# A hybrid encoder step on one core: attention steps moved by units, the router taken token tile by token tile, and a ring of twelve weight buffers for the experts

## The chip, the cores and the metric

One NeuronCore of one Trainium2 chip runs the whole step; the other cores are idle. The metric is the device time of one execution in microseconds (us), the median of several.

## The reference

One layer of a streaming encoder on 512 prompt tokens and 32 sample tokens (544 rows, five token tiles: four of 128 and one of 32), D = 1024, everything in float32.

```python
h = rms_norm(x, p['norm_mix'])
z = h @ p['w_in']                       # qa ka va ra code | qb kb vb | ga gb
...
o_a = rms_norm(o_a, p['gla_norm']) * silu(ra)
u_a = o_a @ p['w_proj_a']
...                                     # 8 heads, softmax1 - lam * softmax2
u_b = o_b @ p['w_proj_b']
mix = sigmoid(ga) * u_a + sigmoid(gb) * u_b
x = x + mix @ p['w_out']
x = x + hmoe(rms_norm(x, p['norm_ffn']), ...)
```

hmoe picks for each token one of 4 groups and in it the best 2 of 4 experts, and adds their weighted outputs (silu(x @ w_gate) * (x @ w_up)) @ w_down, with w_gate and w_up of 1024 x 512 and w_down of 512 x 1024. The outputs are the normalised rows, the new keys and values, and the recurrent GLA state.

## The kernel before, in words

**Arithmetic.** Each fp32 product is three products of reduced-precision parts: every operand is split into a high part, on ScalarE (ACT), and a low part, on VectorE (DVE). three_products (lines 1012 to 1014) does hi x hi, hi x lo and lo x hi on TensorE (PE).

**Units.** layout_of_units writes the projections as a list of units in the order qa, ka, va, ra, qb, kb, vb, ga, gb, pa, pb, wo. A unit is one PSUM bank of output: 24 products of 272 columns for a feature-major stage (128 features by half of the tokens), or two token tiles by 256 columns for va, ra, vb and wo. Weights come in tiles of 256 columns (128 for ga, gb, pa, pb) into a ring of two, and take_apart splits them (lines 697 and 1372). Unit u uses bank u % 3 and waits until unit u - 3 has been evicted.

**Hooks.** hook(u, what) hangs a step behind unit u. Every engine walks the same list of units, and does its part of each hooked step at that place of its own program; so the order on each engine follows from the hook table. Hooked are the GLA steps (gla_in, gla_o, gla_out for token tile i), kout (key rows), the 32 attention slots (head k // 4, query block k % 4) with their later parts up to slot 35, the sample's keys, scores, softmax and values (keys, sscore, soft, mixp, probs, svalue, snorm, sturn), the split of the two attention outputs (oa, ob), the sigmoids (sig) and the first router steps.

**Router.** After wo the rows x2 are normalised (h2, line 1499) and stored to h2_rows in DRAM (POOL, line 643), transposed and multiplied with the router weights. When all five tiles' logits are there, DVE works out group, experts, rank and slot for all tiles at once in some sixty small operations (lines 1609 to 1687), with rank sums (1236, 1238) and a slot table (1245) on PE. From slot_i, POOL gathers each expert's 128 rows by an indirect DMA (line 656).

**Experts.** Each of 16 experts has six weight parts of 1 MB: gate 0 and 1, up 2 and 3, down 4 and 5. SP (the load queue) loads each into the one of six raw slots that belongs to its kind, when DVE has made e_lo of the part before it there. ACT makes e_hi (899, three buffers), DVE e_lo (1696); POOL makes e_lo of the first two parts (652). PE's body(r) does GU (gate and up products) of expert r, AT (transpose of hh) and Dn (down products) of expert r - 1, and XT, the transposes of expert r + 1's rows. ACT copies the result to yo and stores it to y_rows; at the end each token's two rows are gathered (yg), weighted and added, and the last norm follows.

Of the kernel before, what the change touches and what calls it, by code (L numbers as in the profile page):

```python
# [38 lines left out]
NBLK = NE + NOVF  # L39
PARTS, PART, PBUF = 6, KC * FE // 2, 3  # L40
# [4 lines left out]
SLOTS = 4 * DH  # L45

# [5 lines left out]
def layout_of_units():  # L52
# [4 lines left out]
              ("ga", "w_in", C_GA, D), ("gb", "w_in", C_GB, D), ("pa", "w_proj_a", 0, D), ("pb", "w_proj_b", 0, D),  # L57
              ("wo", "w_out", 0, D)]
    tiles, kinds, nth = [], [], []
    for kind, name, col, width in stages:  # L60
        wide = P if kind in NARROW else WC
        for n in range(width // wide):
            tiles.append((name, col + n * wide, wide))
            kinds.append(kind)
            nth.append(n)
# [6 lines left out]
    for n, kind in enumerate(kinds):  # L72
        token_major = kind in ("va", "ra", "vb", "wo")

        parts = [(i, 0) for i in range(0, NTILE, 2)] if token_major else [(f, h) for f in range(tiles[n][2] // P) for h in range(2)]
        for m, (a, b) in enumerate(parts):
            if kind == "ra":
                eng = "A"
            elif kind in ("pa", "pb", "wo"):
# [5 lines left out]
            h = 2 * nth[n] + m - 4  # L85
            if kind == "pa" and 0 <= h < DH:
                add("AD"[h % 2], tile=None, kind="ox", nth=h, a=0, b=0, first=False, last=False, token_major=False)
    return tiles, kinds, units


def build(nc, x_prompt, x_sample, cache_k, cache_v, state_gla, norm_mix, w_in, w_decay, b_decay, gla_norm, w_proj_a,
# [16 lines left out]
    h2_rows = nc.dram_tensor("h2_rows", (NT, D), F32)  # L108
    y_rows = nc.dram_tensor("y_rows", (NBLK * CAP, D), F32)
    h2_rows, y_rows = h2_rows.ap(), y_rows.ap()  # L110

    ctx = ExitStack()
    with ctx:
# [16 lines left out]
        g_diff_s = small[:, 21:22]  # L130
# [51 lines left out]
        dist_s = at("dist_s", AT_X + 4224, [P, PAST + TS])  # L182
        dist = at("dist", AT_X + 8448, [P, TP])
        kbS = at("kbS", AT_X + 10496, [P, DH, TS])
        obs = at("obs", AT_X + 11520, [P, DVB])
        obq = at("obq", AT_X + 12032, [P, DVB])
        head_st = at("head_st", AT_X + 12544, [P, 3, 4 * DH])
        att_st = at("att_st", AT_X + 12928, [P, 4, 8])
# [1601 lines left out]
```

## Time and profile before

| | us |
|---|---|
| median of 3 runs | 1170.91 (1169.93 to 1171.38) |
| the profiled execution's own time | 1172.25 |
| its span in the trace | 1170.3 |
| PE busy | 1034.7 (88%) |
| DVE, ACT, POOL busy | 639.5, 541.4, 141.3 |
| mean granted clock of PE | 0.945 |

The trace is of one execution. A wait is idle time of an engine in front of an instruction, with what ended it. The granted clock is PE's, as a share of full speed. GLA runs until some 300 us, attention from 417 to 585, the sample's attention until some 720, wo from 721, the router from 776, the experts from 830 to 1133.

### The profile page before, as it was taken

The page shows a single profiled execution, that of the slowest core. Times are in us where ns is not written, and L with a number is a line of the kernel's source. Part 1 is how long each engine was busy: PE and PEld are TensorE (multiplying, and loading weights), DVE is VectorE, ACT ScalarE, POOL GpSimd, SP SyncE. Part 2 cuts the span into 40 slices and gives each one's busy share as a digit, 9 for nine tenths or more (in the row PEclk, how much of TensorE's full clock was granted, in tenths as well). Part 3 has the DMA queues.
Part 4 walks back from the last instruction along what each step waited for, and adds up shares of the span by engine and source line. Part 5 has one row for each costly group of instructions (what it writes and reads, how often), then busy time and mean ns, then how long its engine had stood idle before and what let it go on. Part 6 is the DMA issues. An engine that isn't in the chain of part 4 may idle for free.

```text
span 1170.3 us, 17496 instructions
## 1 busy us (share of the span) xinstructions
PE 1034.7 (88%) x7174; PEld 943.2 (81%) x7174; DVE 639.5 (55%) x919; ACT 541.4 (46%) x717; POOL 141.3 (12%) x138
## 2 busy tenths in 40 slices
PE   3999999999999989999789798992599999999940
PEld 2999999887999978888678698992478888888830
DVE  5223821343221146767644465237569889889826
ACT  6225622332122144544644522142367787787722
POOL 3200000200000033422111100003100101100003
PEclk9999999999999999999899898995799999999975
DMA  7863545326364485564343345412489999999736
GB/s 154 255 83 64 67 78 74 55 41 103 64 83 91 77 123 81 47 81 73 122 131 109 99 141 172 189 72 77 159 292 413 412 414 414 413 414 414 278 111 229
DMA packets 125514, 198.01 MB, mean 169 GB/s; under 512 B 10864, under 2 KB 72304, under 8 KB 125440
## 3 DMA queue, kind: packets, MB, share of 16 engines
q1 hardware_dynamic: 112336, 149.37, 48.3%
q0 software_dynamic: 10176, 36.97, 8.6%
q10 hardware_dynamic: 2928, 10.62, 2.3%
q8 instruction: 55, 0.90, 0.3%
q14 instruction: 19, 0.16, 0.0%
HBM read 174.40 MB, written 22.54 MB: 168 GB/s over the span
## 4 chain that ended last, share of the span: by engine, by line
PE 83%; DVE 6%; ACT 4%; DMA 3%; issue 2%; POOL 0%; ACTq 0%; DVEq 0%; POOLq 0%
PE ps L1012 24%; PE ps L1014 23%; PE ps L1013 23%; PE ps L997 5%; PE ps L1143 2%; PE ps L1129 2%; DVE x L1759 1%; DMA ring<-in_w_in_dram 1%; PE ps L1108 1%; PE ps L1076 1%; PE ps L1092 1%; ACT sqa L750 1%; DVE ra L1437 1%; DMA out_dram<-vb 1%; PE ps L1107 1%
## 5 line engine op out<-in xcount | busy, mean ns | idle before, releaser
L1696 DVE TENSOR_TENSOR e_lo<-raw,e_hi 128x2048 fp32r<-128x2048 f32 x94 | 215.0, 2288 | 47.9 <-ACT e_hi L899 47.3
L899 ACT ACTIVATE e_hi<-raw 128x2048 fp32r<-128x2048 f32 x96 | 184.1, 1918 | 70.0 <-PE ps L1014 52.0
L1012 PE MATMUL ps<-h_hi,w_hi 128*128 128x272 f32 x640 | 191.7, 300 | 3.9 <-DVE h_lo L1361 3.9
L1014 PE MATMUL ps<-h_hi,w_lo 128*128 128x272 f32 x640 | 186.9, 292 | 0.0
L1013 PE MATMUL ps<-h_lo,w_hi 128*128 128x272 f32 x640 | 186.7, 292 | 0.0
L1372 DVE TENSOR_TENSOR w_lo<-ring,w_hi 128x2048 fp32r<-128x2048 f32 (+1 forms) x44 | 81.7, 1856 | 105.5 <-ACT w_hi L697 105.5
L697 ACT ACTIVATE w_hi<-ring 128x1024 fp32r<-128x1024 f32 (+1 forms) x60 | 87.2, 1453 | 107.6 <-PE ps L1014 98.1
L1012 PE MATMUL ps<-w_hi,h_hi 128*128 128x256 f32 x480 | 136.1, 284 | 0.0
L1013 PE MATMUL ps<-w_lo,h_hi 128*128 128x256 f32 x480 | 135.7, 283 | 0.0
L1014 PE MATMUL ps<-w_hi,h_lo 128*128 128x256 f32 x480 | 134.7, 281 | 0.0
L1012 PEld LDWEIGHTS ps<-h_hi,w_hi 128*128 128x128 f32 x640 | 123.1, 192 | 5.5 <-DVE h_lo L1361 4.1
L1013 PEld LDWEIGHTS ps<-h_lo,w_hi 128*128 128x128 f32 x640 | 123.2, 192 | 0.2
L1014 PEld LDWEIGHTS ps<-h_hi,w_lo 128*128 128x128 f32 x640 | 122.8, 192 | 0.0
L1012 PE MATMUL ps<-e_hi,x_hi 128*128 128x512 f32 x256 | 104.9, 410 | 7.4 <-DVE hh L1705 5.0
L1014 PE MATMUL ps<-e_hi,x_lo 128*128 128x512 f32 x256 | 101.6, 397 | 0.0
L1013 PE MATMUL ps<-e_lo,x_hi 128*128 128x512 f32 x256 | 101.4, 396 | 0.0
L1012 PEld LDWEIGHTS ps<-w_hi,h_hi 128*128 128x128 f32 x480 | 90.4, 188 | 1.5 <-ACT va L873 1.1
L1014 PEld LDWEIGHTS ps<-w_hi,h_lo 128*128 128x128 f32 x480 | 90.8, 189 | 0.0
L1013 PEld LDWEIGHTS ps<-w_lo,h_hi 128*128 128x128 f32 x480 | 90.2, 188 | 0.0
L1012 PEld LDWEIGHTS ps<-e_hi,x_hi 128*128 128x128 f32 x256 | 49.2, 192 | 18.3 <-DVE hh L1705 5.4
L1014 PEld LDWEIGHTS ps<-e_hi,x_lo 128*128 128x128 f32 x256 | 49.0, 191 | 10.9
L1013 PEld LDWEIGHTS ps<-e_lo,x_hi 128*128 128x128 f32 x256 | 49.4, 193 | 9.0
(349 smaller groups left out, 2020.7 us busy)
## 6 DMA issues: line engine op xcount, KB each, us to landing
raw<-in_w_gate_dram SPq DMA_DIRECT2D x32, 1024.0 KB, 8.8
raw<-in_w_up_dram SPq DMA_DIRECT2D x32, 1024.0 KB, 9.6
raw<-in_w_down_dram SPq DMA_DIRECT2D x32, 1024.0 KB, 8.3
ring<-in_w_in_dram SPq DMA_DIRECT2D x24, 1024.0 KB, 9.3
ring<-in_w_in_dram SPq DMA_DIRECT2D x16, 512.0 KB, 8.6
y_rows<-yo ACTq DMA_DIRECT2D x16, 512.0 KB, 6.0
y_rows<-att POOLq DMA_DIRECT2D x8, 512.0 KB, 13.6
kraw<-in_cache_k_dram POOLq DMA_DIRECT2D x8, 512.0 KB, 8.2
```

The costliest lines, as they stand in the source:

```text
L697: act.activation(piece(w_hi, n), piece(ring, n), ACT.Copy).then_inc(s_hi, 1)
L750: step(act.activation(sqa[0:n], ps[0:n, 5 + h // 2, DV * (h % 2):DV * (h % 2) + DV], ACT.Square, accum_out=stat[0:n, 16 + h:17 + h]))
L899: act.activation(e_hi[:, buf], raw[:, slot], ACT.Copy).then_inc(s_ehi, 1)
L997: last = pe.transpose(out, src, ident[0:ident_n, 0:ident_n])
L1012: pe.matmul(out, left[0], right[0], start=first, stop=False)
L1013: pe.matmul(out, left[0], right[1], start=False, stop=False)
L1014: return pe.matmul(out, left[1], right[0], start=False, stop=final)
L1076: last = pe.matmul(ps[0:n, 5, (NG + NE) * i:(NG + NE) * (i + 1)], h2T[:, i % 2, c, 0:n], wr[:, c], start=c == 0, stop=c == KC - 1)
L1129: last = pe.matmul(ps[:, 3 + a, 0:w], qbT[r, h, P * q:P * q + P], kbT[r, h, 0:w], start=True, stop=True)
L1143: last = pe.matmul(ps[:, 6 + h % 2, DVB * q:DVB * q + DVB], pT[:, k % 2, P * c:P * c + P], vb[:, c, DVB * h:DVB * h + DVB], start=c == 0, ...
L1372: dve.tensor_tensor(piece(w_lo, n), piece(ring, n), piece(w_hi, n).bitcast(F32), ALU.subtract).then_inc(s_lo, 1)
L1696: dve.tensor_tensor(e_lo[:, buf], raw[:, slot], e_hi[:, buf].bitcast(F32), ALU.subtract).then_inc(s_elo, 1)
```

## The change

The first part moves hooks. The second rewrites wo and the router. The third changes the weight ring.

```diff
-            hook(units_of["qb"][3 * i + 1], "gla_out", i)
-            hook(units_of["vb"][2 * i + 1], "kout", i)
-        hook(units_of["vb"][-1], "dist")
+                hook(units_of["qb"][3 * i - 1], "gla_out", i - 1)
+            hook(units_of["vb"][2 * i], "kout", i)
+        hook(units_of["vb"][8], "dist")
...
-        for k in range(SLOTS):
-            hook(gates[k], "slot", k)
+        for k in range(SLOTS + 3):
+            hook((units_of["vb"][-3:] + gates)[k], "slot", k)
+        hook(gates[-2], "oa", 0)
+        hook(gates[-1], "slot", SLOTS + 3)
+        hook(gates[-1], "oa", 1)
         hook(gates[-1], "sig", 0)
-        hook(pa[0], "slot", SLOTS + 2)
-        hook(pa[1], "slot", SLOTS + 3)
-        hook(pa[2], "roots")
+        hook(pa[0], "roots")
```

The sample's steps are spread anew over the 16 units of pa, with the keys in pairs of heads; the sigmoid of gb moves from pa's last unit to pa[12], ob's pieces to pa[10], [11], [13], [14]. dist_s is made later. DVE's wait for the store of vb moves from slot 0 to the rows of head 0 (slot 7). pb's first unit waits for 4 pieces of ob_lo and its second for 6, where the first waited for 6.

wo becomes ten units of one token tile by 512 columns, in the order of WO_ORDER, with w_out in four pieces of 1 MB that have buffers of their own. The router's steps hang behind these units, tile by tile; a step in mid_hooks runs on PE in the middle of the unit.

```diff
+WO_ORDER = [(0, 0), (1, 0), (2, 0), (0, 1), (1, 1), (2, 1), (3, 0), (3, 1), (4, 0), (4, 1)]
...
+        for u, *steps in ((wo[3], ("sq", 0), ("h2", 0)),
+                          (wo[4], ("sq", 1), ("turn", 0), ("logits", 0), ("route", 0), ("h2", 1)),
+                          (wo[5], ("sq", 2), ("turn", 1), ("logits", 1), ("rank", 0), ("slots", 0), ("route", 1), ("h2", 2)),
+                          (wo[6], ("turn", 2), ("logits", 2), ("rank", 1), ("slots", 1), ("route", 2)),
+                          (wo[7], ("sq", 3), ("rank", 2), ("slots", 2), ("h2", 3), ("early", 0)),
+                          (wo[8], ("turn", 3), ("logits", 3), ("route", 3)),
+                          (wo[9], ("sq", 4), ("rank", 3), ("turn", 4), ("slots", 3), ("logits", 4), ("root", 4), ("route", 4), ("rank", 4),
+                           ("h2", 4), ("slots", 4), ("totals", 0))):
...
+            def route(i, n):
...
+                step(dve.max(best[0:n, i], masked))
+                step(dve.max_index(which[0:n], best[0:n, i], masked))
...
+            def slots(i, n):
+
+                dve.wait_ge(s_rank, i + 1)
+                step(dve.tensor_tensor(rt[0:n, 4], ps[0:n, 7, 0:NE], iota_r[0:n], ALU.add))
...
-            for e in range(NE):
-                if e >= 2:
-                    pool.wait_ge(s_xt, e - 1)
-                gather(e, e % 2)
+                for k in range(2):
+                    pool.indirect_dma_start(x_rows, bass.IndirectOffsetOnAxis(slot_i[0:n, k, i:i + 1], 0), h2[i % 2][0:n],
+                                            None).then_inc(s_sc[i % 2], 16)
+
+            def block_in(e, slot):
+                pool.dma_start(xg[:, slot], x_rows[ROWS * e:ROWS * e + CAP]).then_inc(s_xg[slot], 16)
+
+            for i in range(2):
+                pool.wait_ge(s_sc[i], 32 * ((NTILE + 1 - i) // 2))
+            block_in(0, 0)
+            block_in(1, 1)
```

So the normalised rows are scattered, two indirect DMAs a tile, into x_rows in DRAM, where each expert has room for 640 rows (ROWS), and an expert's 128 rows are then one plain load. turn transposes x2 itself, not h2: norm_ffn's gain is multiplied into the router's weights once, for which a small load is added, and the root of the row comes in at route. x_rows is zeroed beforehand by 16 DMAs of 512 KB (the eight y_rows blocks were zeroed before too). What concerns overflowing experts and the final row numbers, overflow() and weights(), stands on DVE after the conversion of part (0, 2). POOL makes no e_lo any more.

```diff
-PARTS, PART, PBUF = 6, KC * FE // 2, 3
+PARTS, PART, PBUF, RAW = 6, KC * FE // 2, 3, 12
...
+            for seq, (e, j) in enumerate(in_order):
+                if seq == 5:
+                    sp.wait_ge(s_unit, wo[8] + 1)
+                elif seq == 9:
+                    sp.wait_ge(s_unit, wo[9] + 1)
+                elif seq >= RAW:
+                    sp.wait_ge(s_part, seq - RAW + 1)
+                load_part(e, j, seq % RAW)
...
-                    dve.tensor_tensor(e_lo[:, buf], raw[:, slot], e_hi[:, buf].bitcast(F32), ALU.subtract).then_inc(s_elo, 1)
+                    dve.tensor_tensor(e_lo[slot][:], raw[slot][:], e_hi[buf][:].bitcast(F32), ALU.subtract).then_inc(s_elo, 1)
```

Parts go through twelve slots in order. e_lo is written over the raw weights of its slot, and a slot is free again when PE has used the part (s_part). Part (0, 0) is converted behind wo[7] ("early").

Three places of the order. First, ScalarE from wo's last weights on; sq is the Square of a row tile, x2T and h2T copies of its transposes. Before:

```order
L697 ACTIVATE w_hi_51<-ring_49 128x2048 [waits s_unit,s_w1]
L821 ACTIVATE sq_123,stat<-x_118 128x1024 [waits s_evD]
L822 ACT_TABLE_LOAD
L822 ACTIVATE stat<-stat,eps 128x1 [waits s_act]
L821 ACTIVATE sq_123,stat<-x_118 128x1024 [waits s_evD]
L822 ACTIVATE stat<-stat,eps 128x1 [waits s_act]
L828 ACTIVATE h2T<-ps 128x1024 [waits s_h2x]
```

Now:

```order
L748 ACTIVATE wo_hi_129<-wo_raw_125 128x2048 [waits s_w1]
L870 ACTIVATE sq_134,stat<-x_119 128x1024 [waits s_evD]
L871 ACT_TABLE_LOAD
L871 ACTIVATE stat<-stat,eps 128x1 [waits s_act]
L870 ACTIVATE sq_134,stat<-x_119 128x1024 [waits s_evD]
L871 ACTIVATE stat<-stat,eps 128x1 [waits s_act]
L877 ACTIVATE x2T<-ps 128x1024 [waits s_h2x]
L870 ACTIVATE sq_134,stat<-x_119 128x1024 [waits s_evD]
L871 ACTIVATE stat<-stat,eps 128x1 [waits s_act]
L877 ACTIVATE x2T<-ps 128x1024 [waits s_lgm,s_h2x] x2
```

The order of squares and copies is the old one, but these steps now lie between wo's units and not behind them.

Second, ScalarE at the passage from gb to pa; mixT at L776 and L822 is sigmoid 0, head_st the roots, kcT the copies of sample keys. Before:

```order
L718 ACTIVATE oa_hi<-fmA 128x1088 x3
L855 ACTIVATE pT<-ps 128x512 [waits s_pvq,s_px]
L776 ACT_TABLE_LOAD [waits s_evD]
L776 ACTIVATE mixT<-mixT 128x2176 [waits s_evA]
L776 ACTIVATE mixT<-mixT 128x2176
L835 ACTIVATE ob<-ps 128x512 [waits s_row,s_pvq]
L697 ACTIVATE w_hi_51<-ring_49 128x1024 [waits s_unit,s_w0]
L787 ACTIVATE kcT<-ps 128x512 [waits s_kcx] x4
L779 ACT_TABLE_LOAD
L779 ACTIVATE head_st<-head_st,eps 128x32 [waits s_row]
```

Now:

```order
L894 ACTIVATE ob<-ps 128x512 [waits s_row,s_pvq]
L864 ACTIVATE oa_hi<-fmA 128x4x272 [waits s_unit,s_oaT]
L864 ACTIVATE oa_hi<-fmA 128x4x272
L822 ACT_TABLE_LOAD [waits s_evD]
L822 ACTIVATE mixT<-mixT 128x2176 [waits s_evA]
L822 ACTIVATE mixT<-mixT 128x2176
L825 ACT_TABLE_LOAD
L825 ACTIVATE head_st<-head_st,eps 128x32 [waits s_row]
L833 ACTIVATE kcT<-ps 128x512 [waits s_kcx] x2
L738 ACTIVATE w_hi_51<-ring_49 128x1024 [waits s_unit,s_w0]
```

The roots moved ahead of the key copies, and the last outputs of attention (pT, ob) ahead of sigmoid 0.

Third, DVE at the first expert. Before:

```order
L1686 CAST ovi<-ovb 128x8 [waits s_dve]
L1687 CAST ovi<-ov 128x1 [waits s_dve]
L1696 TENSOR_TENSOR e_lo<-raw,e_hi 128x2048 [waits s_ehi,s_elo,s_ovi]
L1700 TENSOR_TENSOR x_lo<-ps,x_hi 128x1024 [waits s_xhi]
L1696 TENSOR_TENSOR e_lo<-raw,e_hi 128x2048 [waits s_ehi]
L1700 TENSOR_TENSOR x_lo<-ps,x_hi 128x1024 [waits s_xhi]
```

Now, the last of 46 small operations that stand between e_lo(0, 2) and e_lo(0, 3):

```order
L1776 CAST ysl<-ybase 128x10 [waits s_dve]
L1724 TENSOR_REDUCE rs<-rs 128x5 [waits s_ge]
L1725 RECIPROCAL rs<-rs 128x5 [waits s_dve]
L1726 TENSOR_SCALAR rs<-rs 128x5 [waits s_dve]
L1727 RECIPROCAL rs<-rs 128x5 [waits s_dve]
L1728 TENSOR_TENSOR rs<-rs 128x5 [waits s_dve]
L1729 TENSOR_TENSOR rs<-rs 128x5 [waits s_dve]
L1610 TENSOR_TENSOR e_lo_153<-raw_141,e_hi_162 128x2048 [waits s_ehi,s_dve]
L1780 TENSOR_TENSOR x_lo<-ps,x_hi 128x1024 [waits s_xhi]
```

The overflow work moved from in front of e_lo(0, 2) to behind it.

## Rows read from the trace of the kernel before

**Rows 1.** Waits of TensorE (PE), whole span. Columns: us in total, times, longest us.
```profile
PE ps L1236 <- DVE chosen L1634: 13.3, 1, 13.3
PE ps L1245 <- DVE ysl L1677: 9.6, 2, 7.0
PE ps L997 <- DVE ra L1437: 7.6, 5, 2.6
...
PE ps L997 <- DMA xg<-h_rows,slot_i: 4.9, 1, 4.9
...
PE ps L1129 <- DVE att_st L1529: 3.1, 1, 3.1
```
**Rows 2.** Stretch; length; busy of PE, PEld, DVE, ACT, POOL; PE clock; DMA share; GB/s.
```profile
200.00:230.00 30.00, 27.40 (x196) 26.52 (x196) 9.53 (x17) 9.11 (x20) 6.27 (x15) 0.94 0.40 76
420.00:424.00 4.00, 4.00 (x22) 3.99 (x21) 1.65 (x8) 2.13 (x7) 2.31 (x1) 0.59 0.98 43
562.00:592.00 30.00, 22.13 (x127) 19.76 (x125) 15.03 (x25) 18.34 (x23) 4.41 (x5) 0.77 0.40 123
592.00:660.00 68.00, 61.14 (x653) 54.77 (x652) 38.22 (x77) 32.38 (x50) 7.03 (x8) 1.00 0.35 109
660.00:678.00 18.00, 10.85 (x69) 10.64 (x68) 5.20 (x12) 8.17 (x9) 5.43 (x16) 0.72 0.59 211
718.00:728.00 10.00, 6.86 (x36) 6.67 (x35) 4.49 (x7) 2.67 (x3) 0.00 (x0) 0.66 0.51 164
```
**Rows 3.** Chain that ended last: start us, us, what; wo to expert 4.
```profile
718.22 3.14 issue
...
821.69 4.31 DMA xg<-h_rows,slot_i
826.04 1.98 PE ps L997 x8
...
830.39 0.80 PE ps L1012
...
850.23 0.80 PE ps L1012
...
875.60 0.87 PE ps L997 x8
893.34 0.87 PE ps L997 x8
```
**Rows 4.** Expert stage: columns of rows 2, then ScalarE's (ACT) longest wait.
```profile
900.00:1080.00 180.00, 180.00 (x854) 149.44 (x853) 160.48 (x92) 144.81 (x103) 14.47 (x9) 1.00 1.04 413
...
ACT e_hi L899 <- PE ps L1014: 27.4, 43, 0.8
```
**Rows 5.** Lines, 552 to 800: busy us, mean ns of one | idle before.
```profile
L776 ACT ACTIVATE mixT<-mixT 128x2176 f32<-128x2176 f32 x2 | 3.9, 2014 | 0.0
...
L776 ACT ACT_TABLE_LOAD x2 | 2.6, 1283 | 0.0
```
**Rows 6.** Lines, 760 to 832 (router), same columns.
```profile
L1499 DVE SCALAR_TENSOR_TENSOR h<-x,stat,gffn 128x1024 f32<-128x1024 f32 x4 | 5.1, 1284 | 0.1
...
L821 ACT ACTIVATE sq<-x 128x1024 f32<-128x1024 f32 x4 | 4.2, 1051 | 18.7 <-DVE x L1571 18.7
...
L656 POOL DMA_INDIRECT xg<-h_rows,slot_i x3 | 3.1, 1021 | 21.5 <-DVE slot_i L1679 17.1 <-PE ps L997 4.2 <-issue 0.3
```
**Rows 7.** Lines, 900 to 1080 (experts), same columns.
```profile
L1696 DVE TENSOR_TENSOR e_lo<-raw,e_hi 128x2048 fp32r<-128x2048 f32 x62 | 141.8, 2288 | 19.5 <-ACT e_hi L899 19.2
...
L656 POOL DMA_INDIRECT xg<-h_rows,slot_i x9 | 14.5, 1608 | 145.0 <-PE ps L997 145.0
```
**Rows 8.** DMA issues: out<-in, queue, count, KB each, median us to landing.
```profile
h_rows<-h POOLq DMA_DIRECT2D x4, 512.0 KB, 2.9
```
**Rows 9.** Experts' end: columns of rows 2, then a wait of ScalarE.
```profile
1112.00:1133.00 21.00, 14.26 (x50) 10.70 (x48) 6.91 (x5) 5.99 (x6) 0.00 (x0) 0.76 0.33 126
...
ACT e_hi L899 <- DMA raw<-in_w_down_dram: 6.4, 2, 5.0
```

More of the change, by code:

```diff
@@ new lines, in build @@
+        e_lo = [at(f"e_lo{k}", a, [P, PART], F32R) for k, a in enumerate(raw_at)]
+        e_hi = [at(f"e_hi{k}", a, [P, PART], F32R) for k, a in enumerate((181248, 143360, AT_H))]
+        xg = at("xg", AT_H + 8192, [P, 2, D])
+        x_hi = at("x_hi", AT_H + 16384, [P, 2, KC, P], F32R)
+        x_lo = at("x_lo", AT_H + 24576, [P, 2, KC, P], F32R)
+        hh_hi = at("hh_hi", AT_H + 32768, [P, FE // P, P], F32R)
+        hh_lo = at("hh_lo", 189440, [P, FE // P, P], F32R)
+        hh = at("hh", 151552, [P, 2, FE])
@@ L380, in build @@
[L380 to L391 removed]
+            hook(pa[2 + h], "normed", h)
@@ L571, in _, with head_bias @@
                 pool.dma_start(dst.rearrange("t h d -> t (h d)"), kb_rows[0:n, i % 2]).then_inc(s_kst[i % 2], 16)
+            def head_bias(h):
+                pool.tensor_scalar(bias[:, h % 2, 0:TP], dist[:], 2.0 ** -(h + 1), None, ALU.mult).then_inc(s_bias, 1)
+            pool.wait_ge(s_bs, 1)
+            head_bias(0)
+            head_bias(1)
+            pool.wait_ge(s_bias, 2)
             emptied(pool, units_of["vb"][-1])
@@ L575, in _ @@
             pool.dma_start(new_v_s[0, 0].rearrange("t h d -> t (h d)"), vb[0:TS, 4]).then_inc(s_vst, 16)
-            def head_bias(h):
-                pool.tensor_scalar(bias[:, h % 2, 0:TP], dist[:], 2.0 ** -(h + 1), None, ALU.mult).then_inc(s_bias, 1)
             def load_keys(g, j):
@@ L671, in _ @@
             pool.wait_ge(s_exdone, 1)
+            pool.wait_ge(s_ovi, 2)
             for i, (t0, n) in enumerate(TILES):
@@ L888, in _ @@
                     act.activation(m_hi[:, f, HALF * b:HALF * b + HALF], tmpm[:, b], ACT.Copy).then_inc(s_mhi, 1)
-                if d["last"] and d["tile"] + RING < len(wtiles):
+                if d["last"] and d["tile"] + RING < first_wo:
                     take_apart(d["tile"] + RING)
@@ L1259, in GU @@
                     c, w = KC // 2 * (j % 2) + i, slice(FE * i, FE * i + FE)
-                    last = three_products(ps[:, j // 2], (x_hi[:, slot, c], x_lo[:, slot, c]), (e_hi[:, buf, w], e_lo[:, buf, w]),
+                    last = three_products(ps[:, j // 2], (x_hi[:, slot, c], x_lo[:, slot, c]), (e_hi[buf][:, w], e_lo[low][:, w]),
                                           c == 0, c == KC - 1)
@@ L1275, in Dn @@
                         w = slice(D * i + 512 * b, D * i + 512 * b + 512)
-                        last = three_products(ps[:, 6 + b], (hh_hi[:, c], hh_lo[:, c]), (e_hi[:, buf, w], e_lo[:, buf, w]),
+                        last = three_products(ps[:, 6 + b], (hh_hi[:, c], hh_lo[:, c]), (e_hi[buf][:, w], e_lo[low][:, w]),
                                               c == 0, c == FE // P - 1)
@@ L1596, in _ @@
                             dve.tensor_copy(dst, src).then_inc(s_ev["D"], 1)
-                if d["last"] and d["tile"] + RING < len(wtiles):
+                if d["last"] and d["tile"] + RING < first_wo:
                     take_apart(d["tile"] + RING)
```

754 lines of the change are left out of this document (400 added, 354 removed).

## Prediction

> **What bounds the kernel now.** I read TensorE's waits over the whole span first [rows 1], then the granted clock by stage [rows 2], the chain that ended last [rows 3] and the expert stage [rows 4]. TensorE is the engine to follow: in the expert stage it is busy for 180.00 of 180 us at full clock while ScalarE's conversions wait for it and no wait for a weight load shows [rows 4]. So time is to be had only where TensorE stands still, and just after, because a stretch with a stall also shows a lower clock: 0.77, 0.72 and 0.66 in the three stretches of the attention tail with most idle time, against 1.00 between two of them [rows 2]. I count a clock loss as busy time x (1 - granted clock) of such a row. The sum is made against the profiled execution, 1172.25 us: span 1170.3 and 1.95 around it, and 1.34 over the median of 1170.91.
>
> **Part 1, GLA.** gla_out(i) stands one unit after gla_o(i) and waits for VectorE's ra five times, 7.6 us together, at most 2.6 [rows 1]. From the expert stage a product of 512 columns takes 0.228 us: one expert's period, 893.34 - 875.60 = 17.74 [rows 3], less 12 transposes of 0.87/8, over 72 products. A qb unit is 24 products of 272 columns, 24 x 0.228 x 272/512 = 2.9. The chain behind it is thus 2.9 + 2.6 = 5.5 long, and the change puts two units, 5.8, over it. The clock loss there is 27.40 x 0.06 = 1.6 [rows 2]. I take 0.4 as left: **-8.8**. What hides the chain is the second qb unit.
>
> **Part 2, attention's start.** Slot 0 waits 3.1 us [rows 1], since DVE stands at the store of vb, and the slow stretch behind costs 4.00 x 0.41 = 1.6 [rows 2]. The change moves that DVE wait to slot 7 and starts three units earlier; what slot 0 then needs (the last key rows, dist, bias 0) was asked for one vb unit before. All of it goes: **-4.8**. The bias tables stand ahead of the vb store in POOL's queue now; the store has seven slots to land.
>
> **Part 3, attention's tail.** The four idle stretches are 30 - 22.13, 68 - 61.14, 18 - 10.85 and 10 - 6.86, 25.0 together; clock loss 22.13 x 0.23 + 10.85 x 0.28 + 6.86 x 0.34 = 10.5 [rows 2]; 35.5 in all. What is late next, by the order of ScalarE (front, second place): the keys come a unit earlier, and besides sigmoid 0 the roots now stand ahead of their copies. Two table loads of 1.28 and two sigmoids of 2.01 [rows 5] are 6.6 us of ScalarE against one pa unit of 2.9, so TensorE's third key transpose waits some 3.4 (6.6 less 2.9, less 0.3 of the unit's end), and a clock loss of 2 follows (the stretches with a stall lose between 1.6 and 5.1 [rows 2]). Half of what the second stretch loses to softmax hand-overs (6.86) stays, 3.8, since scores and softmax are as far apart as before. pb's first unit needs four pieces of ob_lo, not six, the last two units earlier than ScalarE's sigmoid 1 let it: I keep 2.9 of 7.15 and a clock loss of 2. The hand-over from pb to wo is unchanged: 3.1 + 2.8. Left: 5.4 + 3.8 + 4.9 + 5.9 = 20.0, so **-15.5**. Bounds: the stage could keep all 35.5 (0), or only the 5.9 (-29.6).
>
> **Part 4, wo to the first experts.** Before: wo starts at 718.22 + 3.14 = 721.36, the first expert product at 830.39, the transposes of expert 3's rows at 875.60 [rows 3]: 154.2. In it TensorE waits 13.3, 9.6 and 4.9 for routing, slot table and gather [rows 1]. After:
> - Ten units of 24 x 0.228 = 5.47: 54.7, with 2.3 of slow clock at the start as before. Four turns of 0.87 and four logits of 0.9 lie between them: 7.1. Rank products: 0.6.
> - ScalarE's order (front, first place) puts sq(1) ahead of tile 0's x2T copy, and sq(2) ahead of tile 1's. sq(1) waits for unit wo[4] itself, but logits(0) stand right behind that unit and want the copy. So TensorE stands twice for an eviction (0.95), Square (1.05 [rows 6]), its accumulator and Sqrt (0.5) and a copy of as many elements (1.0): 3.6 each, with 1.7 of clock each (1.6 to 5.1 after a stall [rows 2]): 10.6. wo is thus 75.3 long.
> - wo's end to the first expert product, for tile 4: eviction, squares, transposes, copy and logits 4.1; eleven small DVE steps at 0.2 to 0.25 make 6.6; h2 1.28 [rows 6] and four slot steps make 9.0; two scatter issues of 1.02 [rows 6] with 0.25 between make 11.6; no scatter is in this trace: the nearest rows are a plain store of 512 KB, 2.9 [rows 8], and an indirect gather, 4.3 [rows 3]. I take 2.9 for it, as the other write, and 0.5 + 2.9 for the block load: 17.9. Transposes at half clock 2.0 [rows 3], x_hi 1.0, x_lo 1.2 and hand-overs make 22.7. Ends: 2 x 2.9 and 2 x 4.3 for the trips, 22.7 to 25.5.
> - First expert product to expert 1's: 850.23 - 830.39 = 19.8 before [rows 3]. DVE now runs overflow() and weights(), 46 small steps of 0.22, 10.1 us, between e_lo(0,2) and e_lo(0,3) (front, third place). With two e_lo of 2.29 [rows 7], part 3 is ready 14.7 after the start, and TensorE wants it at 12 (three parts, the first at half clock, and a transpose); 2.7 of stall, and 1.7 of later hand-over with hh and a slow clock: 24.3. Then 25.4 to expert 3's transposes, as before.
> Total 75.3 + 22.7 + 24.3 + 25.4 = 147.7; with 0.9 (next sentence) 148.6: **-5.6**.
>
> An indirect issue takes 1.02 with DVE on small steps and 1.61 in the expert stage [rows 6, 7], where DVE is at e_lo nearly always; in the change e_lo(0,1) runs beside the two last scatters, which is worth 2 x 0.6, less what the first has done by then: 0.9. The Trainium skill (SBUF — State Buffer, "Who interferes with whom") says that VectorE and GpSimd lock each other out of a shared port pair, the loser waiting for the whole instruction. Taken by that sentence, the last scatter would wait a full e_lo and the sum would be 1.4 worse than with the row's 0.9.
>
> **Part 5, experts.** The steady stage is bound by TensorE, not by loads [rows 4]: twelve slots instead of six change nothing there, 0. At its end ScalarE waits 6.4 us for the last down parts and yo and silu's products stand behind it; from 1112 to 1133 TensorE idles 6.74 and loses 14.26 x 0.24 = 3.4 [rows 9]. Six more slots, at a part each 17.74/6 = 2.96 us, let those loads be issued up to 17.8 us earlier. Left is the chain over hh_hi and hh_lo, 2.4: **-7.7**.
>
> **At nothing.** 8.4 MB of zeros more are written (16 blocks of 512 KB), hidden under ra and qb, where DMA has a share of 0.37 to 0.40 [rows 2]. S_in stands behind 16 of these issues in POOL's queue but is wanted only at the last GLA step; without that slack this step would wait for it. The extra small gain load, the product with wr and the longer SP list stand far from a due time. The last gathers and norm stay.
>
> **Sum.** -8.8 - 4.8 - 15.5 - 5.6 - 7.7 = -42.4: span 1127.9, execution 1129.9, median about **1128.5**. A change under 0.2% (2.3 us) couldn't be told from none.
>
> **Rivals.**
> 1. The new orders cost less than I read. If x2T and kcT copies aren't late and overflow is covered, 10.6 + 5.4 + 4.4 more go: about **1108**. For it: the stalls are read from the order alone. Against it: both waits are on the unit that is named, whatever the durations. 0.2.
> 2. The hand-overs move instead of going: attention's tail keeps its 35.5 (+15.5), or the two DRAM trips take gathers' 4.3 to 7.3 each, as where weight loads run beside them (+4 to +8). About **1148**. For it: SP issues seven loads around wo's end. 0.23.
> 3. The ring doesn't do what it says: the last down parts come no earlier, because a slot is now freed by TensorE's product, later than by e_lo. Then 7.7 stay: **1136**. Against: twelve slots are 35 us of work, a load and two conversions take under 15. 0.05.
> 4. **Slower.** Expert loads become the bound: the ring keeps more loads, row blocks and stores in flight and the rate falls under what an expert needs. It decides when a period exceeds 17.74 + 42.4/16 = 20.4 us, that is, when 7.34 MB per expert come at less than 360 GB/s; at 340 a period is 21.6 and the time **1190**. Against it: the stage runs at 413 GB/s now and needs no more [rows 4], and loads are issued no sooner than slots free. 0.04. The Trainium skill (SBUF — State Buffer, "A bandwidth-pool intuition that's wrong") gives about 358 GB/s for one core from HBM, by which the kernel before would already take 20.5 a period; the measured 413 [rows 4] decides against that here.
>
> **How the numbers follow.** The sum, with each term off by its own bounds, holds 0.48, from 1118 to 1141. Rival 1 0.2, rival 2 0.23, rival 3 0.05, rival 4 0.04. 1107 to 1150 takes in rivals 1 to 3 up to their outer parts and leaves 0.2 out. Faster by over 0.2%: 0.94, all but rival 4 and some of rival 2; same 0.02; slower 0.04.
>
> **What would show it.** In the profile after: no wait for gla_out's products over 0.5 us; slot 0 without a wait; TensorE waiting for kcT at the first pa units; two waits for x2T of 3 to 4 us behind the fifth and sixth wo unit; 22 to 26 us between wo's end and the first expert product; a wait for e_lo in front of expert 0's fourth part; the steady period at 17.7; no ScalarE wait for the last down parts. The prediction is wrong if the steady period moves, if the tail of attention idles as long as before, or if the block load lands later than 10 us after the last scatter's issue.

## The result and the profile after

The changed kernel takes **1143.72 us** (median of 4 runs, 1143.11 to 1146.84) against 1171.14 for the kernel before on the same chip: ratio 0.9775, 95% interval 0.976 to 0.979. The forecast was 1128.5 with a range of 1107 to 1150: the sign and the range hold, but of 42.4 us only 27.4 came. The time lies outside the 1118 to 1141 that the prediction gave to its own sum; it is in the range because that was stretched for the rivals. The profiled execution has a span of 1142.3, 28.0 less than before.

I first took the start of each stage from the traces: the first product of a stage on TensorE, or expert r's first transpose, and the end of the span. Two kernels of the next section stand beside them, since the question is where the parts of the change act.

| first product of | before | after | a1_att (attention part alone) | r9_all (four mends) |
|---|---|---|---|---|
| qb | 209.95 | 209.03 | 210.06 | 210.28 |
| vb | 348.00 | 337.05 | 338.09 | 338.31 |
| gates | 409.41 | 400.96 | 401.99 | 402.21 |
| pa | 573.03 | 551.44 | 552.33 | 552.54 |
| pb | 667.42 | 637.52 | 639.99 | 631.71 |
| wo | 721.36 | 692.20 | 691.78 | 680.95 |
| expert 0 | 830.39 | 800.54 | 798.66 | 773.68 |
| expert 3, transposes | 875.60 | 852.62 | 844.29 | 818.64 |
| expert 15, transposes | 1088.36 | 1065.47 | 1057.11 | 1031.47 |
| end | 1170.3 | 1142.3 | 1137.7 | 1108.1 |

Before to after: 29.2 us are won by wo's start (29.1 forecast for parts 1 to 3). That this agrees to 0.1 is in part luck: qb and kb give 10.0 where 8.8 were forecast, vb to pb 18.2 where 20.3 were, and 0.9 lie ahead of qb, where the two other kernels of the table win nothing. From wo to expert 3 it takes 160.4 instead of 154.2, so **6.2 are lost where 5.6 were to be won**. From expert 3 to 15 nothing changes (212.8 both times). After that 5.1 are won, where 7.7 were forecast.

TensorE's waits in the changed kernel, the view of [rows 1]; columns: us in total, times, longest.

```profile
PE ps L1039 <- DMA xg<-x_rows: 12.0, 1, 12.0
PE ps L1054 <- issue: 8.6, 2, 6.0
PE ps L1118 <- ACT x2T L877: 7.5, 3, 3.2
PE ps L1054 <- DVE hh L1785: 5.0, 1, 5.0
PE ps L1054 <- DVE e_lo L1610: 4.7, 1, 4.7
...
PE ps L1039 <- DVE obs L1526: 3.8, 1, 3.8
PE ps L1039 <- ACT kcT L833: 2.8, 2, 2.6
PE ps L1122 <- DVE chosen L1589: 2.7, 1, 2.7
```

The waits of [rows 1] for ra, att_st, ysl and the gather are gone, that for chosen is down from 13.3 to 2.7. In their place stand the wait for the scattered rows (12.0), wo's start (the 6.0 of "issue"), three for tokens' transposes (x2T), one for a low weight part (e_lo), and in the attention tail one for the rows of the sample's last heads (obs) and for key copies (kcT).

Stretches of the changed kernel, columns of [rows 2]: a piece of GLA, the pa units up to pb's start, wo, the middle of wo, the expert stage, and the last expert up to the last output copy.

```profile
200.00:230.00 30.00, 30.00 (x219) 28.94 (x218) 11.78 (x20) 11.02 (x21) 12.79 (x18) 1.00 0.93 295
...
551.44:637.52 86.08, 75.67 (x744) 68.80 (x742) 47.45 (x89) 49.94 (x67) 11.22 (x13) 0.96 0.40 123
...
692.00:775.00 83.00, 76.40 (x346) 63.37 (x347) 30.55 (x95) 16.57 (x20) 6.01 (x6) 0.88 0.40 148
724.00:752.00 28.00, 21.73 (x94) 18.36 (x95) 9.54 (x40) 5.73 (x9) 2.05 (x2) 0.76 0.09 38
...
880.00:1060.00 180.00, 180.00 (x853) 149.41 (x852) 160.72 (x93) 144.25 (x102) 4.76 (x9) 1.00 1.04 413
1070.00:1104.45 34.45, 31.82 (x136) 25.62 (x135) 23.94 (x15) 20.37 (x15) 0.00 (x0) 0.95 0.12 46
```

The first row is full now (27.40 of 30 busy before [rows 2]), though the zeroing of x_rows runs beside it with a DMA share of 0.93. The expert row is that of [rows 4]: 180 busy, 413 GB/s. The loss stands in the third and fourth row: wo at a clock of 0.88.

The chain of the changed kernel that ended last, from wo's start to expert 3; columns of [rows 3].

```profile
692.20 0.77 PE ps L1054
...
723.91 0.70 DVE x L1684
724.64 1.16 ACT sq L870 x2
725.82 0.29 ACT stat L871
726.11 0.92 ACT x2T L877
727.08 1.96 PE ps L1118 x16
...
740.34 3.60 PE ps L1118 x16
...
753.27 1.70 PE ps L1118 x16
...
784.32 2.23 POOL x_rows L688
786.55 0.30 issue
786.86 5.50 DMA x_rows<-h,slot_i
792.36 0.29 issue
792.64 3.51 DMA xg<-x_rows
796.20 1.99 PE ps L1039 x8
...
813.78 2.30 DVE e_lo L1610
...
826.41 0.80 PE ps L1054
...
852.62 0.87 PE ps L1039 x8
```

At 723.91 the forecast stall can be read off: eviction, Square, Sqrt, copy, then tile 0's logits. These take 1.70 at full clock, and behind the second stall 3.60, since TensorE then runs at its lower level (0.50 granted, 1.2 GHz).

### The profile page after: what moved, and what is told of

Same layout as the page of the kernel before. It is cut to its first block, busy times and chain, and to the rows that moved or that the text cites. A ratio compares the mean times of both kernels' runs of the same rounds, so it can differ in the third digit from the quotient of the medians.

```text
span 1142.3 us, 16883 instructions
## 1 busy us (share of the span) xinstructions
PE 1028.1 (90%) x6932; PEld 926.3 (81%) x6932; DVE 647.9 (57%) x987; ACT 541.2 (47%) x717; POOL 139.7 (12%) x162
## 4 chain that ended last, share of the span: by engine, by line
PE 83%; DVE 7%; ACT 4%; DMA 3%; issue 2%; POOL 0%; ACTq 0%; POOLq 0%; DVEq 0%
PE ps L1054 24%; PE ps L1055 23%; PE ps L1056 23%; PE ps L1039 5%; PE ps L1197 2%; DMA ring<-in_w_in_dram 2%; PE ps L1183 2%; DVE x L1841 1%; DVE h_lo L1416 1%; PE ps L1118 1%; PE ps L1159 1%; PE ps L1143 1%; PE ps L1158 1%; DVE e_lo L1610 1%; DVE fo L1835 1%
## 5 line engine op out<-in xcount | busy, mean ns | idle before, releaser
L1610 DVE TENSOR_TENSOR e_lo<-raw,e_hi 128x2048 fp32r<-128x2048 f32 x96 | 219.5, 2288 | 37.6 <-ACT e_hi L887 37.2
L1427 DVE TENSOR_TENSOR w_lo<-ring,w_hi 128x2048 fp32r<-128x2048 f32 (+1 forms) x40 | 72.5, 1813 | 105.0 <-ACT w_hi L738 105.0
L738 ACT ACTIVATE w_hi<-ring 128x1024 fp32r<-128x1024 f32 (+1 forms) x56 | 79.5, 1420 | 84.1 <-PE ps L1056 67.2
L1054 PEld LDWEIGHTS ps<-e_hi,x_hi 128*128 128x128 f32 x256 | 49.6, 194 | 23.6 <-DVE hh L1785 5.5
```

Of the source, the lines that this page charges most:

```text
L738: act.activation(piece(w_hi, n), piece(ring, n), ACT.Copy).then_inc(s_hi, 1)
L1054: pe.matmul(out, left[0], right[0], start=first, stop=False)
L1427: dve.tensor_tensor(piece(w_lo, n), piece(ring, n), piece(w_hi, n).bitcast(F32), ALU.subtract).then_inc(s_lo, 1)
L1610: dve.tensor_tensor(e_lo[slot][:], raw[slot][:], e_hi[buf][:].bitcast(F32), ALU.subtract).then_inc(s_elo, 1)
```

## Experiments

My theory after the result (A in most of the runs): the attention part gives what was forecast. Part 4's mechanisms are there, but the change brings four avoidable hand-overs of its own that cost more than the router's better order saves. The rival: the router's new form is slow by itself (two DRAM trips, ten smaller units, contention), and mending hand-overs only moves the waits. Most runs take the changed kernel and mend or undo one thing. The stage pa has the same code in several of these kernels and takes 86.1 to 88.9 in them, at granted clocks of 0.96 down to 0.92 and with the same waits to 0.2 us; so a difference under 3 us in one stage can be scatter of the clock, unless a wait shows it.

### The attention part alone

a1_att is the kernel before with the hooks of GLA, slots and sample, POOL's and the banks' order that belong to them, and nothing of wo, router and ring:

```diff
+            if i:
+                hook(units_of["qb"][3 * i - 1], "gla_out", i - 1)
...
-            hook(units_of["qb"][3 * i + 1], "gla_out", i)
...
-        for k in range(SLOTS):
-            hook(gates[k], "slot", k)
+        for k in range(SLOTS + 3):
+            hook((units_of["vb"][-3:] + gates)[k], "slot", k)
```

> The kernel before with the attention part of the change alone (GLA outputs, slots sooner and spaced by units, attention tail); router, expert tables and ring as before. Theory A (the stage boundaries tell the shares): wo starts some 29 us sooner as in the changed kernel, everything behind it as in the kernel before (wo to the fourth expert's turn 154, the end 82), so about 1142 (1138 to 1146), within 0.3% of the whole change: router and ring together bring nothing net. Rival B (router and ring bring the 13 us that the prediction gave them, and the attention part less than its boundaries show): about 1155. Rival C (the parts disturb each other through the queues, so the attention part alone is better than both): below 1136.

1139.62 us, ratio 0.9736 (0.9719 to 0.9754). That is theory A, and a little more: the interval lies below the whole change's 0.976 to 0.979. **Router and ring as changed don't bring 13 us; they cost about 4.** The table says where: pb to wo 54.7 against 51.8 here, wo to expert 3 160.4 against 152.5, given back in part at the end (76.8 against 80.6). TensorE's waits of a1_att show the old router and the shorter hand-over to wo:

```profile
PE ps L1246 <- DVE chosen L1642: 12.5, 1, 12.5
PE ps L1255 <- DVE ysl L1685: 9.6, 2, 6.9
PE ps L1019 <- issue: 5.3, 2, 3.1
PE ps L1004 <- DMA xg<-h_rows,slot_i: 5.1, 1, 5.1
```

So the change removes 27.2 us of waits for the old routing (chosen, ysl, gather), and puts 12.0, 2.7 and its own stalls in their place, until the stage is longer than it was.

### GLA: gla_out back in its old place

```diff
-            if i:
-                hook(units_of["qb"][3 * i - 1], "gla_out", i - 1)
             hook(units_of["qb"][3 * i - 1] if i else units_of["ra"][-1], "gla_in", i)
             hook(units_of["qb"][3 * i], "gla_o", i)
+            hook(units_of["qb"][3 * i + 1], "gla_out", i)
```

> Edit: gla_out goes back to one unit behind gla_o, the rest of the change stays. Theory A, the GLA spacing alone gives the 10 us that the stretch of qb and kb became shorter: the time rises by 8 to 10, to about 1153, with five waits for VectorE's ra again. Rival, the shorter stretch came from elsewhere (weights, kout's place, clock) and gla_out's waits are hidden by something else: under 1147.

1156.47 (1148.66 to 1157.87), ratio 0.9854 (0.9811 to 0.9896). TensorE's wait returns just as in [rows 1]:

```profile
PE ps L1037 <- DVE ra L1486: 7.6, 5, 2.6
```

qb and kb take 136.6 instead of 128.0, so 8.5 of the 12.7 lie in the stage itself, where 8.8 were forecast. Of these 7.6 are the waits. The clock over the stage stays at 1.00, so that the 1.6 of clock in the forecast's term is not shown to hang on them. Some 0.9 stands before the stage, as much as between other kernels of the table, and 2.8 in pa, which has the same waits at a clock of 0.92 where the changed kernel had 0.96. The four times spread over 9.2 us, so that the 12.7 of the medians is rough, and the 8.5 of the stage is the better figure.

### The attention tail: roots behind the first key copies, sigmoid 1 last

```diff
-        hook(pa[0], "roots")
...
-                (("keys", (0, 0, 0)),),
+                (("keys", (0, 0, 0)), ("roots", 0)),
...
-                (("svalue", 1), ("sig", 1)),
+                (("svalue", 1),),
...
-                (("ob_s", 0), ("ob_s", 1)))):
+                (("ob_s", 0), ("ob_s", 1), ("sig", 1)))):
```

> Edit: in attention's tail the roots go behind the first two key copies and the second sigmoid goes back to pa's last unit. Theory A, ScalarE's tables and sigmoids are what TensorE waits for in this tail: the wait for kcT (2.6) falls to about 1 and the one for obs (3.8) under 1, 4 to 6 us in all, about 1138.5. Rival, the second sigmoid only moves its wait: pb's first units then wait for VectorE's evictions, and the time stays above 1142.

1135.81, ratio 0.9694 (0.9676 to 0.9712). Between 545 and 640 TensorE's waits are now

```profile
PE ps L1053 <- ACT qbT L933: 2.3, 1, 2.3
PE ps L1038 <- DVE scs L1521: 1.1, 1, 1.1
PE ps L1038 <- ACT kcT L832: 1.0, 1, 1.0
...
```

The wait for obs is gone, that for key copies down to 1.0. pa is 79.1 long instead of 86.1. So ScalarE's order (table loads and sigmoids ahead of copies that TensorE wants) was the cause in both places. The prediction had named it for the keys, but not for the sample's rows.

### wo's start: not waiting for pb's last bank

In the changed kernel wo[0] waits for two w_out pieces and for the eviction of pb's very last unit. In r3_wo it waits for the first piece and the last unit but one, the second piece is asked for in the middle of the unit, and that piece is converted one unit later in pb.

```diff
+                if u == wo[0]:
+                    pe.wait_ge(s_lo, n + 1)
+                    emptied(pe, pb[-2])
+                if u == wo[3]:
                     pe.wait_ge(s_lo, n + 2)
-                    if u == wo[0]:
-                        emptied(pe, pb[-1])
...
+                        if u == wo[0] and c == KC // 2:
+                            pe.wait_ge(s_lo, n + 2)
```

> Edit: wo's first unit waits only for the pb unit whose half of the tokens it reads and, in its second half, for the second piece of w_out; that piece's conversion moves behind pb[14]. Theory A, the hand-over's 6.0 us are the last m chain behind the conversion of 1 MB (2.3 on VectorE, 1.9 on ScalarE): the wait falls under 1.5 and the slow clock behind it (3.0) mostly goes; 1143.7 falls by 5 to 8, to about 1137. Rival, the 6.0 are the pb chain itself or the load of w_out: the wait stays over 3 and the time above 1140.

1136.23, ratio 0.9705 (0.9678 to 0.9733). The wait of 6.0 at wo's start is gone (of "issue" 3.1 in all remain, the longest 2.5), pb to wo takes 49.3 instead of 54.7, and wo to expert 0 104.1 instead of 108.3: the second number is clock, since behind a stall of 6 the first products ran slowly (0.43 us a product in place of 0.23).

### The turns ahead of the squares

```diff
-                          (wo[4], ("sq", 1), ("turn", 0), ("logits", 0), ...
-                          (wo[5], ("sq", 2), ("turn", 1), ("logits", 1), ...
+                          (wo[4], ("turn", 0), ("sq", 1), ("logits", 0), ...
+                          (wo[5], ("turn", 1), ("sq", 2), ("logits", 1), ...
```

> Edit: on ScalarE the copy of a tile's transposes (turn) goes ahead of the next tile's Square (sq) behind wo[4] and wo[5]. Theory A, the order of ScalarE makes TensorE wait for x2T and then run at half clock: both waits of 3.2 us go, with the 6.3 us that the clock costs behind them and the half-speed logits, so 1143.7 falls by 10 to 13 us, to about 1132. Rival, the copy isn't what holds TensorE there: VectorE's eviction and route come next in the chain and a wait for chosen or x2T takes their place; less than 4 us gained, above 1139.

1131.85, ratio 0.9663 (0.9644 to 0.9682). wo to expert 0 takes 95.6 instead of 108.3: 12.7 in this stage, 11.9 by the medians, for an edit that moves two copies. The middle of wo, which stood at 21.73 busy and 0.76 above, is now

```profile
724.00:752.00 28.00, 28.00 (x160) 24.15 (x160) 15.04 (x70) 6.65 (x12) 4.25 (x5) 1.00 0.19 76
```

Of the 12.7, 6.4 are the waits for x2T (7.5 to 1.1) and 5.2 the clock behind them (21.73 x 0.24). The stalls in wo cost nearly twice their length here.

### VectorE at the first expert, and the last scatter

r2_ovf puts overflow() and weights() ahead of expert 0's x_out, into the time in which the rows are on their way. r6_lock also takes e_lo(0, 1) from beside tile 4's scatters and puts it behind that work; its edit is the one shown.

```diff
-            part_lo(part_of(0, 1))
...
-            x_out(0, 0)
-            part_lo(part_of(0, 2))
             overflow()
             weights()
+            part_lo(part_of(0, 1))
+            x_out(0, 0)
+            part_lo(part_of(0, 2))
```

> Edit: overflow() and weights(), 46 small VectorE operations, run before x_lo of expert 0, in the 10 us in which VectorE waits for the scatters and the first block load, and not between e_lo(0,2) and e_lo(0,3). Theory A, they delay expert 0's fourth part: its wait of 4.7 us goes and some clock with it; first expert product to expert 3's transposes falls from 52.1 to about 46, total about 1138. Rival, hh's chain sets the pace there anyway, so that its wait of 5.0 grows as the other goes: above 1142. Second rival, the small operations end later than x_hi and push x_lo back: slower than 1143.7 by up to 2.

> Edit: overflow() and weights() ahead of expert 0's x_lo as in the run with only that edit (1137.5), and besides e_lo(0,1), of 2.29 us, behind them and not beside the last tile's scatters. Theory A, VectorE's operation with two inputs holds up the building of the scatter on GpSimd (the first of the two took 2.23 us, the eight before it 0.95 to 1.12): it falls to about 1.0, the rows land 1 to 1.3 us sooner and the time is 1 to 2 us under 1137.5. Rival, the 2.23 has to do with the scatter itself (32 rows, its buffer): it stays over 2 and the time within 1 of 1137.5.

r2_ovf: 1137.49, ratio 0.9709 (0.9688 to 0.9731); TensorE's wait of 4.7 for e_lo is gone. r6_lock: 1134.89, ratio 0.9696 (0.9676 to 0.9716); the wait for the first block goes from 12.1 to 10.6. These 1.5 are what e_lo's place gives; the two intervals overlap, and the rest of the 2.6 between the medians is not shown to come from it (the clock in wo was 0.93 in this trace and 0.89 in that of r2_ovf). The rows of VectorE and POOL around tile 4's scatters in the changed kernel (start, us, engine, line, operation):

```profile
783.44 2.27 DVE L1610 TENSOR_TENSOR e_lo<-raw,e_hi 128x2048 fp32r<-128x2048 f32 x1
```
```profile
784.32 2.23 POOL L688 DMA_INDIRECT x_rows<-h,slot_i  x1 [4.36 <-DVE slot_i L1603]
786.86 0.86 POOL L688 DMA_INDIRECT x_rows<-h,slot_i  x1 [0.30 <-issue]
```

and POOL's in r6_lock:

```profile
783.36 0.86 POOL L688 DMA_INDIRECT x_rows<-h,slot_i  x1 [4.36 <-DVE slot_i L1603]
784.53 0.85 POOL L688 DMA_INDIRECT x_rows<-h,slot_i  x1 [0.31 <-issue]
```

In the changed kernel e_lo ends at 785.71 and the issue beside it at 786.55, 0.84 later, which is what an undisturbed issue takes in all (0.86). So it did not run slowly: it stood until e_lo had ended. One such issue would be little, but the kernel before has eleven more, its gathers in the steady expert stage. Each started inside an e_lo and ended 0.80 to 0.82 after that e_lo did, as here (e_lo ends at 895.20, the issue at 896.01):

```profile
892.91 2.29 DVE L1696 TENSOR_TENSOR e_lo<-raw,e_hi 128x2048 fp32r<-128x2048 f32 x1 [1.20 <-ACT e_hi L899]
```
```profile
894.48 1.53 POOL L656 DMA_INDIRECT xg<-h_rows,slot_i  x1 [16.06 <-PE ps L997]
```

A gather that had started 0.17 ahead of an e_lo (823.16) took 0.96, as without one. The Trainium skill (SBUF — State Buffer, "Who interferes with whom") describes it so: a VectorE instruction with both inputs in SBUF keeps a GpSimd operation that reads SBUF out for the whole instruction. The traces agree: a held issue ends 0.80 to 0.84 after the subtraction, and one by itself takes 0.86 (scatter) or 0.96 (gather). The same section of the Trainium skill infers that building a DMA's descriptors is not held by such a subtraction; for an indirect DMA these runs show that it is.

### The ring: twelve slots, but loads six ahead

```diff
-                    sp.wait_ge(s_part, seq - RAW + 1)
+                    sp.wait_ge(s_part, seq - 6 + 1)
```

> Edit: SP loads a part only when the part six before it has been used, so that at most six are ahead in the steady stage; the twelve slots stay. Theory A, the last down parts were late because loads ran only about six parts ahead: the wait of ScalarE for the last down parts comes back and 3 to 6 us with it, 1147 to 1150, with the steady period still 17.74. Rival 1, the gain at the end came from the new order of loads and not from their number: under 1145. Rival 2, six parts ahead of use (17.7 us) are too few for a load of 8.5 us and ScalarE's lead of three parts (8.9 us): the period rises above 18 and the time above 1152.

1142.95, ratio 0.9758 (0.9742 to 0.9775): as the whole change. Theory A is out, and rival 2 with it. Nothing of the end's gain is lost (expert 15's transposes to the end 76.5, against 76.8 with twelve ahead and 81.9 before; the profiled execution took 1147.48, with a clock of 0.93 in pa). ScalarE now does wait for loads, in short pieces of which TensorE sees next to nothing (one period of the steady stage is 0.4 longer):

```profile
ACT e_hi L887 <- DMA raw<-in_w_gate_dram: 8.1, 12, 1.2
ACT e_hi L887 <- DMA raw<-in_w_up_dram: 5.3, 8, 1.0
```

So the number of slots is not what helps. SP's last four loads point to what does; before, in the changed kernel, and in r5_ring6 (start, us, count):

```profile
1093.11 20.42 SPq L480 DMA_DIRECT2D raw<-in_w_down_dram  x4
```
```profile
1056.82 9.05 SPq L516 DMA_DIRECT2D raw<-in_w_down_dram  x4
```
```profile
1078.34 9.02 SPq L516 DMA_DIRECT2D raw<-in_w_down_dram  x4
```

Before, every kind of part had one slot of its own, so that expert 15's two down parts had to wait for the low halves of expert 14's, though the gate and up slots beside them had nothing more to take: 20.42 for four issues. Counted from expert 15's transposes the last was issued at about +25. In r5_ring6 any slot takes the next part in order, the four go out in 9.02, the last at about +18. a1_att, with the old ring, has the same 20.42 and 80.6 to the end, so of the 5.1 gained there 3.8 are the ring's and 1.3 are not. That it is the common order is read from the code and these rows; no run gave each kind its own slots again.

### All together, and the trips

r8_best has r1_turn, r3_wo and r6_lock in one kernel; r9_all adds r7_sig.

> Edits together: copies ahead of squares behind wo[4] and wo[5], overflow() and e_lo(0,1) moved as above, wo's first unit waiting for its own half. If the three gains lie one behind the other on TensorE's path they add up: 1143.7 - 11.9 - 6.2 - 7.5 - 1 = about 1117. Rival, part of a gain only makes room for the next wait (routing of the last tile, or the clock that falls during it): 1120 to 1126.

> The changed kernel with all the mends at once: token turns first, overflow and weights ahead of x_out with the first low parts behind them, wo's first unit not waiting for pb's last bank, and the roots and the second sigmoid moved in the attention tail. Theory A (the losses lie in different stages and add): 1117.4 less the tail's 7.9, about 1109.5 (1107 to 1112). Rival B (the sigmoid behind the last output rows now delays wo's start, which the earlier hand-over made nearer): 1112 to 1117, and a PE wait at wo's start that was gone comes back.

1117.38, ratio 0.9542 (0.9525 to 0.9559), and **1109.03**, ratio 0.9466 (0.9451 to 0.948). The losses add nearly as they should if each lies in a stage of its own: the four single gains make 36.1 by the medians, together they give 34.7. The rival is out: waits mended here don't come back elsewhere. wo's start to expert 3's transposes is 137.7 in r9_all, against 160.4 and, before, 154.2.

The largest wait behind the head of the kernel is then the one for the first block (10.7), whose scatter takes 5.4. r10_hold makes SP's loads from the tenth part on wait for that block; r11_xout then puts x_out(0, 0) ahead of e_lo(0, 1).

```diff
                 elif seq == 9:
                     sp.wait_ge(s_unit, wo[9] + 1)
+                    sp.wait_ge(s_xg[0], 16)
```

> r9_all with one wait more on SP: the weight loads from the tenth part on wait for the first block of rows (they were issued right behind wo's last unit, and filled the DMA engines while tile 4's scatter and the first block load were on their way: 5.4 and 3.7 us). Theory A (these two trips are long because weight loads are ahead of them): scatter 3.3 and block load near 2.5, TensorE's wait for the first block 10.7 -> 7 to 8.5, and about 1106 (1104.5 to 1107.5) against 1109.0. Rival B (the trips are that long by themselves): wait unchanged, 1109, if the held loads still come in time. Rival C (the expert stage needs nearly all the rate that the loads get, so the 15 us in which none is under way aren't made up): the trips are shorter but ScalarE waits for raw weights and TensorE behind it in the first experts, time 1109 to 1120.

1108.76, ratio 0.9479 (0.9465 to 0.9492): no different from r9_all. But the trips did get shorter, by POOL's rows of r9_all

```profile
759.94 0.86 POOL L687 DMA_INDIRECT x_rows<-h,slot_i  x1 [0.30 <-issue]
765.61 1.15 POOL L691 DMA_DIRECT2D xg<-x_rows  x2 [4.80 <-DMA x_rows<-h,slot_i]
```

and of r10_hold:

```profile
758.55 0.86 POOL L688 DMA_INDIRECT x_rows<-h,slot_i  x1 [0.30 <-issue]
761.38 1.14 POOL L692 DMA_DIRECT2D xg<-x_rows  x2 [1.97 <-DMA x_rows<-h,slot_i]
```

From the last scatter's issue to the block's it is 2.8 instead of 5.7. TensorE's waits of r10_hold say where that went:

```profile
PE ps L1039 <- DMA xg<-x_rows: 7.7, 1, 7.7
PE ps L1054 <- DVE x_lo L1782: 5.2, 1, 5.2
```

3.0 less for the block, 2.8 more for x_lo, which stands behind VectorE's last small steps and a low part. None of the three theories had this; ScalarE waited for no load, so the held loads did come in time. Beside the trips the DMA share is 1.04 in r9_all and 0.40 here.

> r10_hold with expert 0's x_lo ahead of the low part of its second weight part on VectorE (in r10_hold the block landed 3 us sooner, but x_lo stood behind a queue of VectorE: the last small steps and a low part of 2.3 us, so that TensorE waited 5.2 for x_lo instead of 2.4). Theory A (what the earlier block gave was taken by VectorE's queue, nothing else): TensorE's wait for x_lo 5.2 -> about 2.9, the second low part still in time, and about 1106.4 (1105 to 1107.5) against 1108.8. Rival B (the part converted later is the next wait: TensorE stands for e_lo within expert 0): a wait for e_lo of 1 to 3, time within 1 of r10_hold.

1105.80, ratio 0.9441 (0.9428 to 0.9453), with a wait of 3.0 for x_lo and none for e_lo in the first expert. The wait does what theory A said, but that the time follows from it is not shown: from wo's start to the end the trace takes 425.9 where r10_hold's takes 426.1. wo to expert 0 is 1.8 shorter, expert 0 to 3 is 1.3 longer, at a clock of 0.87 where it was 0.90. Most of the difference between the two traces lies in pa, which the edit doesn't touch (77.6 at a clock of 1.00, against 79.0 at 0.98). By its median this is the fastest kernel run here, 5.6% under the kernel before and 3.3% under the change.

## Why the prediction was right in sign and 15 us off

- **Part 1, GLA (-8.8): right in its mechanism.** qb and kb together are 10.0 shorter in the changed kernel, and putting gla_out back costs 8.5 there, 7.6 of it the waits. The 1.6 of clock in the term is open: r4_gla has the waits without a lower clock.
- **Parts 2 and 3, attention (-4.8 and -15.5): near, as a sum.** vb, gates, pa and pb are 18.2 shorter, by the table, where the sum has 20.3 (in a1_att 19.7). Two of the terms that stay don't follow from their rows: half of 6.86 is 3.4, not 3.8, and the clock at wo's start is 6.86 x 0.34 = 2.3, not 2.8. No wait is left at slot 0. What was to be late next came: 2.6 for kcT (5.4 with its clock loss was counted). The softmax hand-overs, of which 3.8 was to stay, are down to 1.1, but waits of 3.8 for obs and 2.3 for a bank that ScalarE copies out (qbT) stand there that I had not seen. pb's first wait for ob_lo, 7.1 before, is gone, where I kept 2.9.
- **"The hand-over from pb to wo is unchanged: 3.1 + 2.8": wrong.** It grew to a wait of 6.0. wo's first unit waited for pb's last eviction before, too; a unit of 512 columns also needs two pieces of w_out, and VectorE's conversion of the second (2.29 us from 686.27 on) stands ahead of pb's last evictions. r3_wo removes the wait, a1_att keeps the old 3.1. Within the sum to wo's start, this hid that the rest of the attention part did better than forecast.
- **Part 4, "wo is thus 75.3 long": the step that failed most, 83.0.** The row of wo gives the split. Idle 83.00 - 76.40 = 6.6, where two stalls of 3.6 were forecast. Clock 76.40 x 0.12 = 9.2, where 5.7 were. Busy at full clock 67.2, where 62.4 were: four logits at 1.70, not 0.9, are 3.2 of these 4.8; the rest I didn't assign. The two stalls behind wo[4] and wo[5] came as read from the order, 3.2 each (the four pieces named for the 3.6 make 3.5).
- **wo's end to expert 0: 25.3, not 23.6.** The last scatter landed after 5.50, not 2.9; the row I took was a plain store with no weight loads beside it. r10_hold shows that loads were the reason.
- **Expert 0 to expert 1: 25.9, not 24.3.** The wait for e_lo(0, 3) came at the right place, 4.7 long instead of 2.7. From there to expert 3 26.2, not 25.4.
- **Part 5 (-7.7): -5.1, of which the ring's share is 3.8, and for another reason.** "Six more slots let those loads be issued up to 17.8 us earlier": they are, but six ahead do as well. By SP's rows it is the common order of the slots that counts. Of the 2.6 that are missing, 1.8 are in the row of the last expert: idle 2.6, nearly as counted (2.4), and 1.6 of clock (31.82 x 0.05), which I had left out.
- **At nothing:** the zeroing of x_rows is hidden, as the first stretch shows. The steady period is unchanged.

The four differences of part 4 are 7.7 + 1.7 + 1.6 + 0.8 = 11.8, part 5's is 2.6: that is the error of the sum, 14.4 us by spans. Of the rivals, number 2 gave nearly the measured time (1148), but that is luck: of its two mechanisms one was wrong, since attention's tail did not keep its idle time, and the other, long trips beside weight loads, is right but small (without the loads TensorE waits 3.0 less for the block in r10_hold, and the time is no shorter). Number 1, that x2T, kcT and overflow would not hold TensorE up, is out: all three waits came, and r1_turn, r7_sig and r2_ovf, which mend them, gain 11.9, 7.9 and 6.2 by the medians. Number 3 is out: the last down parts are asked for 25 us sooner, counted from expert 15's transposes. Number 4 is out, with 413 GB/s before and after.

## What to carry to other kernels

When a chain (square, copy, transpose) is moved from behind a loop into it, its old order on each engine becomes a queue: put what the busiest engine waits for first, and what only feeds a later sum behind. Here that was two swapped steps for 11.9 us, and the stalls of TensorE cost nearly twice their length, since the products behind it ran at the lower clock. Measure the parts of a combined change apart: this one gained 2.3%, yet its router and ring were a loss of 0.4%, and after three mends a gain of 2.0% (r8_best's 0.9542 over a1_att's 0.9736).

## What the runs showed of the hardware that I had not expected

- An indirect DMA's issue on GpSimd that starts inside a VectorE subtraction with two operands in SBUF ends 0.80 to 0.84 us after that subtraction has, in the changed kernel and in eleven gathers of the kernel before; moved out of it, it takes 0.86. From a mean (1.61 in [rows 7]) this looked like a slow-down.
- A scatter of tile 4 is 128 KB (32 rows of 4 KB). From its issue to that of the block load behind it, it is 5.7 us with weight loads in flight (r9_all, DMA share 1.04) and 2.8 with these held back (r10_hold, 0.40). The Trainium skill (DMA: Bandwidth & Descriptors, "Anatomy of one DMA — SWDGE (gpsimd) path") gives a fit by which it would be 2.3, an estimate from that page; the runs agree within 0.5 only where the loads are held back.
- Loads held back for 15 us ahead of the expert stage cost nothing there: in r10_hold ScalarE shows no wait for them, though the stage draws 413 GB/s. What it could draw at most no run here shows.
